# A hybrid decoder step on one core: last position of the mix reordered, the expert phase's placing, tail scatters and final fetches moved

## What is computed

```python
u = rmsnorm(x, norm_mix) @ w_in
m = concat(swa_with_sinks(u), gated_deltanet(conv(u)))      # the "mix"
h = x + m @ w_out
hn = rmsnorm(h, norm_ffn)
# router: 8 groups, best group; 8 experts in it, best two; 64 experts in all
g_sel = argmax(softmax(hn @ w_router_group) + b_rg)
e_loc = top_k(softmax((hn @ w_router_expert)[g_sel]) + b_re, 2)
# each expert on its own tokens, in blocks of at most 128 rows
y[token] += gate * ((silu(xb @ w_gate[e]) * (xb @ w_up[e])) @ w_down[e])
out = rmsnorm(h + y, norm_final)
```

## Time and profile before

| | |
|---|---|
| median of 3 runs | 2533.24 us (2531.8 to 2533.3) |
| the profiled execution | 2535.84 us, its span 2534.0 us |
| PE busy | 2251.6 us, 89% of the span |
| DVE, ACT, POOL busy | 1343.1, 651.4, 660.0 us |
| mean granted TensorE clock | 0.948 of 2.4 GHz |
| DMA | 405.30 MB, 160 GB/s over the span |
| stages | mix ends at 1701.6 us, first expert product at 1747.47, last one ends at 2437.5, last scaling at 2527.9 |

### The profile page before, as it was taken

How to read it: one execution, slowest core, us unless ns; L and a number is a source line. 1 busy time by engine, 2 the same in 40 slices (tenths; PEclk the granted TensorE clock), 3 DMA queues, 4 the chain that set the end, 5 groups by cost and what they waited for, 6 DMA issues and landing times. The chain is left out here.

```text
span 2534.0 us, 36266 instructions
## 1 busy us (share of the span) xinstructions
PE 2251.6 (89%) x12560; PEld 1262.6 (50%) x12560; DVE 1343.1 (53%) x2789; ACT 651.4 (26%) x1695; POOL 660.0 (26%) x820
## 2 busy tenths in 40 slices
PE   7999999998958999899999999965699999999940
PEld 4454454433436666666766666643244444444410
DVE  4415235223324655354665656626467677776658
ACT  3202113012114454344445544420000001000012
POOL 1010100100200100210122031213455555555455
PEclk9999999999988999899999999986899999999975
DMA  8041130310166111112311113117599999999947
GB/s 291 26 138 34 43 112 13 106 44 12 53 192 163 58 57 49 48 53 77 103 58 58 57 58 113 41 48 281 209 364 371 364 374 373 376 374 373 351 171 312
DMA packets 172071, 405.30 MB, mean 160 GB/s; under 512 B 51219, under 2 KB 92931, under 8 KB 147321
## 3 DMA queue, kind: packets, MB, share of 16 engines
q1 hardware_dynamic: 142439, 350.39, 38.9%
q0 software_dynamic: 23648, 35.19, 3.9%
q10 hardware_dynamic: 5842, 17.80, 1.8%
HBM read 345.11 MB, written 94.80 MB: 174 GB/s over the span
## 5 line engine op out<-in xcount | busy, mean ns | idle before, releaser
L3099 PE MATMUL p_ps<-p_w_arena,p_x_arena 128*128 128x512 f32 x1024 | 454.4, 597 | 33.5 <-DVE p_x_arena L3000 33.5
L869 PE MATMUL p_ps<-p_xt,p_w 128*128 128x512 f32 x1088 | 476.7, 596 | 0.5 <-DVE p_xt L700 0.5
L3099 PEld LDWEIGHTS p_ps<-p_w_arena,p_x_arena 128*128 128x128 f32 x1024 | 196.1, 192 | 281.2 <-issue 269.9
L869 PEld LDWEIGHTS p_ps<-p_xt,p_w 128*128 128x128 f32 x1088 | 205.0, 191 | 255.4 <-issue 250.2
L2779 POOL DMA_INDIRECT p_x_arena<-s_hn,p_slot x272 | 275.7, 1014 | 121.6 <-issue 73.5
L2427 PE MATMUL p_ps<-p_w_out,p_mixt 128*128 128x512 f32 x544 | 251.8, 607 | 0.0
L3022 DVE STREAM_TRANSPOSE p_y_arena<-p_y_arena 32x64 f32<-32x64 f32 x1024 | 240.8, 235 | 13.2
L3108 PE MATMUL p_ps<-p_w_arena,p_y_arena 128*128 128x512 f32 x512 | 230.2, 592 | 3.2 <-DVE p_y_arena L3022 3.2
L3108 PEld LDWEIGHTS p_ps<-p_w_arena,p_y_arena 128*128 128x128 f32 x512 | 97.2, 190 | 126.0 <-issue 126.0
L3000 DVE STREAM_TRANSPOSE p_x_arena<-p_x_arena 128x1024 f32<-128x1024 f32 x66 | 133.8, 2028 | 37.3 <-DMA p_x_arena<-s_hn,p_slot 35.4
L2427 PEld LDWEIGHTS p_ps<-p_w_out,p_mixt 128*128 128x128 f32 x544 | 99.2, 192 | 105.4 <-issue 103.2
(11 more groups left out here) (419 smaller groups left out, 3066.6 us busy)
## 6 DMA issues: line engine op xcount, KB each, us to landing
p_w_arena<-in_w_exp_gate SPq DMA_DIRECT2D x64, 1024.0 KB
p_w_arena<-in_w_exp_up SPq DMA_DIRECT2D x64, 1024.0 KB
p_w_arena<-in_w_exp_down SPq DMA_DIRECT2D x64, 1024.0 KB
p_w_arena<-s_y SPq DMA_DIRECT2D x16, 1024.0 KB, 13.5
p_x<-in_x_prompt SPq DMA_DIRECT2D x30, 512.0 KB, 4.8
p_w<-in_w_in SPq DMA_DIRECT2D x4, 2048.0 KB
p_spread<-s_roots SPq DMA_DIRECT2D x16, 512.0 KB
s_kv<-p_us SPq DMA_DIRECT2D x32, 256.0 KB
```

What stands on the lines that cost most here:

```text
L869: ins = mm(ps[:, job % 4, :], w[:, c, at:at + P], xt[s % 2][:, c, :], start=(c == 0), stop=(c == KC - 1))
L3099: t = mm(ps[:, 2 + b, :], xt[b][:, c, :], w_gu[bw][:, :, c, :], start=(c == 0), stop=(c == KC - 1))
```

## The change

It has four parts.

1. In the last position of the mix, `output_norm(16)` goes ahead of `layer_sum(15, 1)` on DVE. On PE `turn_hn(15)` and `logits(15)` leave the loop body; after it stand `turn_mix(16)`, the first column half of `project(16)`, `turn_hn(15)`, the second column half, `logits(15)`, `turn_hn(16)`, `logits(16)`. ACT and DVE follow.
2. POOL's eight placings no longer stand ahead of the blocks: after the gather and scatter of each of the first eight blocks comes one placing, written out ahead of the loop. POOL's wait for all of the placing is gone. SP writes out the loads of blocks 8 to 11 ahead of its wait for the placing; its loop starts at 12, and what it no longer loads of `s_h` goes into the last load (four tiles instead of three).
3. In the last loop, POOL's order is scatter 0, gather_listed 0, scatter 1, gather_listed 1, scatter 2, scatter 3, gather_listed 2, gather_listed 3.
4. SP loads `gain` behind the first two fetches of the final sum instead of ahead of them.

```diff
@@ ScalarE, end of the mix
-                if back:
+                if back and front:
                     turned_hn(t - 1)
                     logits(t - 1)
                 if front:
                     level(t + 1, NL)
             turned_mix(NQ - 1)
+            turned_hn(NQ - 2)
             layer_square(NQ - 1)
+            logits(NQ - 2)
             turned_hn(NQ - 1)
             logits(NQ - 1)
@@ VectorE, the loop of the mix
+                if not front:
+                    output_norm(t)
                 if back:
                     layer_sum(t - 1, 1)
...
-                if back:
+                if back and front:
                     turned_hn(t - 1)
-                output_norm(t)
-                if front:
+                if front:
+                    output_norm(t)
                     level_update(t + 1, 4)
...
-            for n in two:
-                layer_sum(NQ - 1, n)
+            layer_sum(NQ - 1, 0)
+            turned_hn(NQ - 2)
+            layer_sum(NQ - 1, 1)
             layer_norm(NQ - 1)
             turned_hn(NQ - 1)
@@ TensorE, end of the mix
-                if back:
+                if back and front:
                     turn_hn(t - 1)
...
-                if back:
+                if back and front:
                     logits(t - 1)
...
             h_ready.after(pe, NQ - 2)
+            lg_ready.after(pe, NQ - 3)
             turn_mix(NQ - 1)
+            for part in two:
+                project(NQ - 1, 0, part)
+            turn_hn(NQ - 2)
+            for part in two:
+                project(NQ - 1, 1, part)
+            h_ready.after(pe, NQ - 1, 1)
+            logits(NQ - 2)
+            turn_hn(NQ - 1)
             lg_ready.after(pe, NQ - 2)
-            for n in two:
-                for part in two:
-                    project(NQ - 1, n, part)
-            turn_hn(NQ - 1)
             logits(NQ - 1)
@@ SyncE, experts
-            for b in ring:
-                load_weights(R + b, R + b, b)
+            for j in range(R, 3 * R):
+                load_weights(j, j, j % R)
             sp.wait_ge(K["ids_out"], 16 * 2 * TILES)
             sp.wait_ge(on["owner_ready"], 1)
...
-            with sp.Fori(2 * R, NE - R, R) as i:
+            with sp.Fori(3 * R, NE - R, R) as i:
...
-            early = NE // R - 3
+            early = NE // R - 4
...
             sp.wait_ge(on["experts_stored"], 1)
-            sp.dma_start(gain, A["norm_final"].unsqueeze(0).to_broadcast([P, D])).then_inc(on["tail_in"], 16)
...
-            for t in range(CB):
+            for t in two:
+                fetch(t)
+            sp.dma_start(gain, A["norm_final"].unsqueeze(0).to_broadcast([P, D])).then_inc(on["tail_in"], 16)
+            for t in range(2, CB):
                 fetch(t)
@@ GpSimd, experts
-            for n in range(2 * n3):
+
+            def place(n):
                 pool.wait_ge(K["ids_out"], 16 * (2 * LAST[0] + n))
...
-            pool.wait_ge(K["ids_out"], 16 * 2 * TILES)
-            with pool.Fori(0, NE - R, R) as i:
+
+            def step(i, b):
+                gather(i + b + R, b)
+                scatter(i + b, b % 2, 8 * i + 16 * (b // 2) + 16, 8 * i + 16 * ((b + 1) // 2) + 16)
+
+            for j in range(2 * R):
+                step(j - j % R, j % R)
+                place(j)
+            with pool.Fori(2 * R, NE - R, R) as i:
                 for b in ring:
-                    gather(i + b + R, b)
-                    scatter(i + b, b % 2, 8 * i + 16 * (b // 2) + 16, 8 * i + 16 * ((b + 1) // 2) + 16)
+                    step(i, b)
             total = n_blocks(pool)
             with pool.Fori(NE - R, total, R) as i:
                 for b in ring:
                     scatter(i + b, b % 2, 8 * i + 16 * (b // 2) + 16, 8 * i + 16 * ((b + 1) // 2) + 16)
+                    if b < 2:
+                        gather_listed(i + b + R, b, 20 * (i + (R - NE)) + 80)
+                for b in (2, 3):
                     gather_listed(i + b + R, b, 20 * (i + (R - NE)) + 80)
```

More of the change, by code:

```diff
@@ L2724, in _ @@
             h_flat = h_all[:].rearrange("p t d -> p (t d)")
-            with sp.Fori(2 * R, NE - R, R) as i:
+            with sp.Fori(3 * R, NE - R, R) as i:
                 for b in ring:
                     load_weights(i + b, i + b, b)
-                sp.dma_start(h_flat[:, bass.ds(i * (D // R) + (-2 * D), D)], S["h"][bass.ds(i * (P // R) + (-2 * P), P)]
+                sp.dma_start(h_flat[:, bass.ds(i * (D // R) + (-3 * D), D)], S["h"][bass.ds(i * (P // R) + (-3 * P), P)]
                              ).then_inc(on["h_in"], 16)
@@ L3046, in _ @@
             dve.wait_ge(on["tail_in"], 32)
-            dve.wait_ge(on["h_in"], 16 * (NE // R - 1))
+            dve.wait_ge(on["h_in"], 16 * (NE // R - 2))
             def add(t):
```

## The result

The changed kernel takes **2494.2 us** (median of 4 runs, 2490.2 to 2502.0) against 2533.3 before, a ratio of 0.985 with a 95% interval from 0.9825 to 0.9877: 39 us faster. The forecast was 2495.7 us with a range from 2489 to 2508.

What follows compares the result with a forecast made beforehand. The experts were taken as bound by TensorE, transfers just behind, so only waits from step order could be won: 9.0 + 24.3 + 4.2 = 37.5 us off the profiled 2535.84, and 2.6 to the median, gave 2495.7 us, range 2489 to 2508.

Steps and rivals of the forecast that it cites:

- Part 1: End of the mix: the early norm and new TensorE order shorten its waits; -9.0 us, bounds -6.2 to -10.7.
- The -0.9 behind them: End of the mix: after a shorter pause the eight transposes take 1.09 us instead of 1.97.
- Part 2: Early experts: TensorE's 22.43 us pause for block 4's rows and 1.89 of slow product go; -24.3 us, at least -20.
- The margin of some 10 us: Early experts: block 4's gathered rows are there some 10 us before their turn.
- the step: GpSimd in the early experts: gather 6.0, scatter and index copy 2.1, placing 1.3, under a block's 10.3 us.
- Parts 3 and 4: Last block to first scale: GpSimd's earlier finish brings the first scale forward; -4.2 us, bounds -2.7 to -6.6.
- Its work is the same as before: Tail: GpSimd, still running two passed-by listed gathers, ends at 2458.7 as before; first scale at 2460.8 instead of 2465.06.
- the sign that it named as wrong: Last loop: a last scatter later than 4 us after the third would show the forecast wrong.
- Placings queue behind the scatters: Rival, early experts: a placing behind a scatter takes 13 us, TensorE loses 12 us, total 2507.7; chance 0.14.
- The transfers become the bound: Rival, experts: without the pause DMA keeps up only 330 GB/s, kernel 19 us slower at 2552; chance 0.03.
- The placing's wait only changes its place: Rival, experts: block 12's late weights or another wait take most of the pause, half of part 2 goes, 2508; chance 0.05.
- The tail gives all or nothing: Rival, final sum: DVE starts at once, 2493.3, or late gain leaves nothing of part 3, 2499.9; chance 0.12 together.

Runs made afterwards that it cites:

- the additions held: Changed kernel with gain awaited at VectorE's first scale, plus VectorE's first addition held until GpSimd finished its late listed gathers: 2498.3 us, 0.9877 of the kernel before.
- two placings a step: Changed kernel with the eight placings two to a step behind the first four steps, not one behind each of eight: 2509.7 us, 0.9896 of the kernel before.
- the norm behind: Changed kernel with VectorE's output norm of the last mix position back behind the layer norm of the one before: 2501.5 us, 0.9899 of the kernel before.

## Why the prediction was right

- **Part 1, -9.0.** -8.4 and -8.9 to the first expert product in the two profiles of the changed kernel, -7.7 there and -9.5 timed alone. From the window products' end to `turn_hn(16)` the forecast had 20.8 us, and it is 20.4. The four parts of the projection took 14.16 us (14.1 forecast), the pause 3.03 (1 to 3), the eight transposes 1.09. The -0.9 behind them was -0.7 at the router products (24.3 instead of 33.5 us after the mark), and 0.3 to 0.7 us were lost again before the first expert product.
- **Part 2, -24.3.** -25.4 and -25.2 in the two profiles of the changed kernel, -24.4 with the placing alone. The gap went whole, and so did the slow product behind it. Placings waited for nothing. The margin of some 10 us, read from the earlier trace rows, measured 12.7. Of the step, 9.4 us forecast, GpSimd made one per 10.3 us, held back by its scatters. SyncE's delay was 8 us, not 12, and cost nothing.
- **Parts 3 and 4, -4.2.** The right mechanism, GpSimd setting the first scale, but the size at the low bound of 2.7: -2.7 and -2.2. The step that failed is "Its work is the same as before", with GpSimd free at 2458.7, which is 24.9 us after the start of the last down product. It is free 27.6 us after it. 1.9 us of that is scatter 63, which goes at 7.1 and not at 5.2 us: GpSimd idles 4.74 us for an output that the forecast had ready at 4.4 us, and that was ready at 6.1, because of the slow last product (in the second profile at 6.2, where VectorE turned rows of a further block ahead of its copy). 0.9 us are operations stretched beside VectorE's additions (20.5 us from scatter 63 to the end of the gathers; 19.6 in the forecast and 19.55 with the additions held). Against these, the first root took 1.0 us and not 2.0. The slow product is chance: in the second profile of the same kernel it took 3.67 us. Where neither delay came up, in the run with the norm behind, whose tail is the same, scatter 63 went at 5.4 and the first scale came at 26.9 us, 4.3 ahead of before. The forecast had the last two scatters 3.6 us apart; they are 5.96, 4.1 in the second profile and 4.5 in that run, so the sign that it named as wrong, more than 4, came up. Alone, this part gained nothing, which lies outside its bounds: they had nothing for the stretched operations, nor for the idle time of 3.21 us. That the gain's place costs nothing behind GpSimd is shown by two runs.
- **Not foreseen:** the end of the span comes 2.2 us later after the last scale. That was so in all nine kernels with the new placing (9.6 to 9.8 us, 11.2 with two placings a step) and in none of the three without (7.3 to 7.4). The last store lands 2.9 us after its issue in both. Behind it the engines meet once more before they clear the semaphores, each with a DRAIN instruction ahead of the meeting. In the kernel before SyncE's comes last, right behind the store's landing; in the changed one it is GpSimd's, and the others go on within 0.2 us of its end. These are GpSimd's drains of before and of the changed kernel, from the view of their line (shortest, median and longest in ns, then the first and last start):

```profile
L2589 POOLq DRAIN  x1: 2396/2396/2396, 2526.0 to 2526.0; - x1
L2599 POOLq DRAIN  x1: 7299/7299/7299, 2489.9 to 2489.9; - x1
```

The drain takes 7.3 us in every kernel with one placing a step, 8.9 with two, and 2.4 to 2.8 in the three without. It starts 4.8 us ahead of the last store's landing in all of them, so that it is over before the landing in the kernel before and 2.5 us after it in the changed one. Why it takes longer stays open.

The rivals: *Placings queue behind the scatters* is refuted in its size; behind a scatter they landed in 6.2 to 8.5 us (two placings a step), not 13. The ring order that the prediction cites for this rival stands in the Trainium skill (DMA: Bandwidth & Descriptors, Queues, rings and completion order) under the queues of SP and ACT, not GpSimd's, and no term of the sum hangs on it. *The transfers become the bound* did not happen, with 374 GB/s over 100 us as before, and 395 for 20. *The placing's wait only changes its place* and both forms of *The tail gives all or nothing* are out for the changed kernel, in which the tail gave part; alone it gave nothing, but not for a late `gain`. That the total came within 1.5 us is in part luck: +0.6 in the mix, -1.1 in the placing, +1.5 in the tail and +2.2 at the end come to 3.2 us too little by the marks, while the timed difference came out 39 us instead of 37.5, within the scatter of the part ahead of them.

## What to carry to other kernels

A chain of small dependent transfers that stands in a block ahead of what feeds TensorE cost nothing here when it was dealt out one to a step of 10.3 us, and 16 us when it was dealt out two to a step; measure that margin before dealing more. When one engine's late start has two causes, such as a transfer and another engine's leftover work, look at both before moving either: here the edits gave some 0 and 4 us alone, and some 7 together. Before starting VectorE's long two-input operations earlier, see whether GpSimd still has small ones to do that the start of VectorE's own chain waits for.

## What the runs showed of the hardware

- VectorE's additions of 1.28 us (128x1024, two inputs in SBUF) stretched GpSimd's operations on up to 128x4 elements from 0.2 us to between 0.93 and 1.24 us, in three runs; with the additions held, those of the gathers were all at 0.27 or less.
- A DMA of 128 small elements took 5.1 us in the mean (3.1 to 6.3) until the next could go where no scatter was under way (DMA share 0.81 over these 36 us), and 6.2 to 8.5 us right behind a scatter.
- Behind an idle time of 4.34 us TensorE's first 16 products took 8.73 us instead of 7.03 to 7.13, with a granted clock of 0.80 over them.
- Behind one and the same idle time of 3.23 us, 8 products took 3.67 us in eight profiles and 5.09 to 6.53 us in five; in the profile shown the granted clock was 0.50 over two of these us, and in the run with the norm behind, at 3.67 us, it stayed at 1.00.
- GpSimd's drain at the end of the program took 2.4 to 2.8, 7.3 or 8.9 us, and with it the time from the last landing to the end 3.1, 5.4 to 5.5 or 7.0 us.
